# Moving six gathers and six adds from the end of a two-layer decoder kernel into its last expert pass, and reordering two steps of its mixers

## The reference, cut to what matters

```python
for l in range(2):
    hn = rmsnorm(h, norm1_g[l]);  u = hn @ w_in[l]                       # 1024 -> 1536
    pool = (window_means(u[:, :512]) - u[:, :512]) @ pool_w[l] * scale   # windows 2, 4, 8, 16
    v = u[:, 512:1024] * sigmoid(u[:, 1024:])
    conv = silu(layernorm(depthwise_conv31(v) + b)) @ conv_pw_w[l]
    h = h + concat(pool, conv) @ w_out[l]
    hn = rmsnorm(h, norm2_g[l])
    if l == 0: h = h + (silu(hn @ wg) * (hn @ wu)) @ wd                  # dense
    else:                                                               # top 2 of 8 experts
        h = h + sum(gate[e] * (silu(hn @ wg[e]) * (hn @ wu[e])) @ wd[e] for e in top2)
y = rmsnorm(h, final_norm_g)      # and the last 15 and 30 rows of the two mixers' inputs
```

## Time and profile before

| | us |
|---|---|
| median of three runs | 1496.43 |
| the profiled execution | 1495.54 |
| its span | 1493.8 |
| PE busy in the span | 1461.5 |
| DVE busy | 1182.0 |
| ACT busy | 915.1 |
| POOL busy | 202.1 |

### The profile page before, as it was taken

The page is one execution under the profiler, slowest core; times in us unless marked ns, Lnnn a source line. Parts: engine busy times, 40 slices in busy tenths (PEclk is TensorE's granted clock), DMA queues, the critical chain, the costliest instruction groups (busy, mean ns, idle before and its releaser), DMA issues.

```text
span 1493.8 us, 21275 instructions
## 1 busy us (share of the span) xinstructions
PE 1461.5 (98%) x7895; PEld 1263.8 (85%) x7895; DVE 1182.0 (79%) x976; ACT 915.1 (61%) x740; POOL 202.1 (14%) x224
## 2 busy tenths in 40 slices
PE   8999999999999999999999999999999999999995
PEld 7879999999979977888888888888888888888884
DVE  4888655544686688888888888888888888888887
ACT  4253433333224587777777777777777777777773
POOL 1465000002344047500000000000000000000002
PEclk9999999999999999999999999999999999999997
DMA  7556996353284399999999999999999999999993
GB/s 203 159 188 207 334 286 198 95 173 113 64 253 161 119 364 400 384 395 377 390 364 385 386 361 384 379 379 382 374 382 371 376 385 361 382 388 370 382 379 113
DMA packets 249680, 453.56 MB, mean 304 GB/s; under 512 B 9605, under 2 KB 99781, under 8 KB 249631
## 3 DMA queue, kind: packets, MB, share of 16 engines
q1 hardware_dynamic: 245056, 442.33, 83.4%
q0 software_dynamic: 2960, 9.73, 2.0%
q10 hardware_dynamic: 1615, 0.85, 0.2%
HBM read 426.51 MB, written 26.37 MB: 303 GB/s over the span
## 4 chain that ended last, share of the span: by engine, by line
PE 66%; DVE 2%; ACT 1%; issue 1%; DVEq 0%; ACTq 0%
PE ps L1676 21%; PE ps L1674 21%; PE ps L1675 21%; PE ps L2044 2%; ACT w_hi L512 0%; PE ps L2034 0%; PE ps L2023 0%; DVE w_lo L517 0%; PE ps L1921 0%; PE ps L1757 0%; DVE yt L1656 0%; PE ps L2112 0%; DVE w_lo L1312 0%; PE ps L2113 0%; PE ps L1872 0%
## 5 line engine op out<-in xcount | busy, mean ns | idle before, releaser
L517 DVE TENSOR_TENSOR w_lo<-raw,w_hi 128x2048 fp32r<-128x2048 f32 x336 | 764.5, 2290 | 117.6 <-ACT w_hi L512 116.3
L512 ACT ACTIVATE w_hi<-raw 128x2048 fp32r<-128x2048 f32 x334 | 639.5, 1915 | 123.4 <-PE ps L1676 122.2
L1676 PE MATMUL ps<-w_hi,xg_lo 128*128 128x512 f32 x896 | 351.4, 392 | 0.0
L1674 PE MATMUL ps<-w_hi,xg_hi 128*128 128x512 f32 x896 | 350.9, 392 | 0.0
L1675 PE MATMUL ps<-w_lo,xg_hi 128*128 128x512 f32 x896 | 350.7, 391 | 0.0
L1675 PEld LDWEIGHTS ps<-w_lo,xg_hi 128*128 128x128 f32 x896 | 168.3, 188 | 37.2
L1674 PEld LDWEIGHTS ps<-w_hi,xg_hi 128*128 128x128 f32 x896 | 168.3, 188 | 36.7 <-DVE w_lo L517 0.2
L1676 PEld LDWEIGHTS ps<-w_hi,xg_lo 128*128 128x128 f32 x896 | 168.3, 188 | 36.1
L1674 PE MATMUL ps<-x_hi,w_hi 128*128 128x336 f32 x580 | 186.3, 321 | 5.9 <-DVE x_lo L1176 2.5
L1675 PE MATMUL ps<-x_lo,w_hi 128*128 128x336 f32 x580 | 183.6, 317 | 0.0
L1676 PE MATMUL ps<-x_hi,w_lo 128*128 128x336 f32 x580 | 182.9, 315 | 0.0
(11 more groups left out here) (283 smaller groups left out, 1576.1 us busy)
## 6 DMA issues: line engine op xcount, KB each, us to landing
raw<-in_moe_w_gate_dram SPq DMA_DIRECT2D x112, 1024.0 KB, 7.2
raw<-in_moe_w_up_dram SPq DMA_DIRECT2D x112, 1024.0 KB, 7.4
raw<-in_moe_w_down_dram SPq DMA_DIRECT2D x112, 1024.0 KB, 7.3
raw<-in_w_in_dram SPq DMA_DIRECT2D x11, 1024.0 KB, 5.2
raw<-in_ffn_w_gate_dram SPq DMA_DIRECT2D x11, 1024.0 KB, 6.0
raw<-in_ffn_w_up_dram SPq DMA_DIRECT2D x11, 1024.0 KB, 6.4
raw<-in_w_out_dram SPq DMA_DIRECT2D x8, 1024.0 KB, 7.7
obuf<-ones SPq DMA_DIRECT2D x15, 512.0 KB, 7.9
```

The source lines that it names most:

```text
L512: nc.scalar.activation(hi, r, ACT.Copy).then_inc(hi_done, 1)
L517: nc.vector.tensor_tensor(lo, r, hi.bitcast(F32), ALU.subtract).then_inc(lo_done, 1)
L1674: nc.tensor.matmul(out, a_hi, b_hi, start=start, stop=False)
L1676: return nc.tensor.matmul(out, a_lo, b_hi, start=False, stop=stop)
```

## The change

There are three edits. First, SP no longer increments `o_early`; POOL itself waits for `o_stored` (with the number of overflow chunks read into a register), issues the six gathers, and then does the six multiplications by the gates and six additions to `yt`, each as an instruction of its own on 112 x 1024 elements; DVE's six `add_gathered` are gone. Second, both halves of the fourth sample part (`conv_samples(3)`) stand ahead of the split of the last `w_in` slot, and the split of the pool maps' weights (`S_POOL_W`) moves behind the centring. Third, PE does the first six of the eight contraction steps of both outputs of slot `S_OUT` ahead of the last two pool maps, and the last two steps behind them.

```diff
@@ sync, behind the last weight load
             sp.wait_ge(o_stored, n_pass * 16 + 16)
-            sp.sem_inc(o_early, 1)
             store_tiles(sp, 0)
@@ gpsimd, at the end of its program
+            n_over = pool.value_load(eids[0:1, 6:7], min_val=0, max_val=5)
+            pool.wait_ge(o_stored, n_over * 16 + (NE * 16 + 16))
+            pool.sem_inc(o_early, 1)
             pool.wait_ge(o_early, 1)
             for i in (0, 1):
                 for t in range(3):
                     gather_outputs(i, t, og_landed[i][t])
+            for i, gates in enumerate((out_gate[:, 0], early_gate)):
+                for t in range(3):
+                    pool.wait_ge(og_landed[i][t], 16)
+                    link(nc.gpsimd.tensor_scalar(og[:, i, t, :], og[:, i, t, :], gates[:, t:t + 1], None, ALU.mult))
+                    nc.gpsimd.tensor_tensor(yt[:, t, :], yt[:, t, :], og[:, i, t, :], ALU.add).then_inc(y_added, 1)
+                    pool.wait_ge(y_added, 3 * i + t + 1)
@@ vector, mixer_layer
                 pool_in(4, 1)
-                conv_samples(3, (0,))
+                conv_samples(3)
...
                 low_half(0, pool_half_lo)
                 low_half(1, lo_done)
                 split_at[0] = n + 1
-                conv_samples(3, (1,))
-                split_to(b + S_POOL_W)
                 dve.wait_ge(sums_done, SUMS[("mean", l)] + 1)
@@ vector, at the end
-            def add_gathered(i, t, gates):
-                dve.wait_ge(og_landed[i][t], 16)
-                if i:
-                    dve.wait_ge(y_added, t + 1)
-                nc.vector.scalar_tensor_tensor(yt[:, t, :], og[:, i, t, :], gates[:, t:t + 1], yt[:, t, :],
-                                               ALU.mult, ALU.add).then_inc(y_added, 1)
...
-            for t in range(3):
-                add_gathered(0, t, out_gate[:, 0])
-            out_low(0)
-            add_gathered(1, 0, early_gate)
-            out_low(1)
-            for t in (1, 2):
-                add_gathered(1, t, early_gate)
+            for i in (0, 1):
+                out_low(i)
             dve.wait_ge(y_added, 6)
@@ tensor, mixer_layer
+                split_ready(b + S_OUT)
+                w_hi_0, w_lo_0 = dense_slot(b + S_OUT, 256)
+                first_outs = [group(("wout", l, i)) for i in (0, 1)]
+
+                def first_part(ks):
+                    for k in ks:
+                        pe.wait_ge(evac, GROUP[("pool", l, k) if k < NG else ("pw", l, k - NG)] + 1)
+                        for i in (0, 1):
+                            cols = slice(P * i, P * (i + 1))
+                            ins = mm3(first_outs[i][:, 0:T], w_hi_0[:, k, cols], w_lo_0[:, k, cols], m_hi[:, k, :], m_lo[:, k, :],
+                                      k == M_ORDER[0], k == M_ORDER[-1])
+                            if k == M_ORDER[-1]:
+                                ins.then_inc(mm_done, 1)
+
+                first_part(M_ORDER[:2 + KC])
                 for g in POOL_ORDER[2:]:
                     pool_map(g)
+                first_part(M_ORDER[2 + KC:])
...
-                for s in range(4):
+                for s in range(1, 4):
...
-                            if s == 0 and i == 0:
-
-                                pe.wait_ge(evac, GROUP[("pool", l, k) if k < NG else ("pw", l, k - NG)] + 1)
...
-                    if l == 1 and s:
+                    if l == 1:
```

## The result

| | before | after |
|---|---|---|
| median of the runs, us | 1496.58 | 1512.85 (1511.61 to 1515.08) |
| ratio, 95% interval | | 1.0113 [1.0101, 1.0125] |
| the profiled execution, us | 1495.54 | 1511.61 |
| its span, us | 1493.8 | 1509.8 |

The account below looks back on a forecast made before the run. PE was taken to bound the expert passes, with DVE having 23.3 us in 200 to spare. Last pass 12.4, mixers 2.6 and end 0 took the profiled 1495.54 to 1510.5, a median of 1511.4 (own range 1506 to 1517).

Parts of the forecast that it names:

- The sign and the size: Whole kernel: slower, median 1511.4 us; chance of slower 0.88, same 0.06, faster 0.06.
- A pass bound by PE gives nothing back: Last expert pass: the 12.4 us that PE waits for delayed splits are lost in full.
- The main term: Last pass: POOL's 18.4 us of sums hold up DVE's splits, so PE waits 12.4 us (bounds 8 and 17).
- The gathers: Last pass: gathers moved there make weight slots land some 6.5 us late, stalling about 2.3 us alone (bounds 0 and 4).
- I add nothing for it: Last pass: the gathers' 2.3 us fall where DVE is late already, so they add nothing to the 12.4.
- Output slot: Mixers, output slot begun ahead: waits of 0.7, 0.7 and 2.1 us replace 1.06; loss 2.4 a layer (bounds 0.5 and 3.5).
- Sample part: Mixers, fourth sample part: PE's wait of 1.22 us goes; gain 1.1 us a layer (0.8 to 1.22).
- End: End of the kernel: removing DVE's six adds gains 0 (bounds: gain 0.4, loss 0), as they were hidden behind PE.
- Rival 1: Last pass: POOL loses every arbitration and works only in DVE's idle time; 1503.9 us; chance 0.11.
- Rival 2: Last pass: sums cost DVE next to nothing, the gathers' lateness decides; 1501.3 us; chance 0.08.
- Rival 3: Last pass: PE's clock falls to 1.2 GHz while it starves, some 15 us more; 1526 us; chance 0.07.
- Rival 4: Whole kernel: sums run beside DVE, weights land in time, mixers gain both waits, end 0.4; 1491.7 us; chance 0.06.

Follow-up runs that it names:

- adds_only: Kernel before plus six POOL additions of 112 x 1024 on free tiles in the last pass, no multiplications, gathers and DVE's adds at the end: 1503.69 us, ratio 1.0051.
- end_edit: Kernel before with the whole first edit (gathers and sums on POOL in the last pass, DVE's adds gone), mixers as before: 1505.72 us, ratio 1.0070.
- gathers_early: Kernel before with only the six gathers moved into the last pass, issued by POOL; DVE adds at the end as before: 1499.90 us, ratio 1.0039.
- half_gathers: Kernel before with three of the six gathers moved into the last pass, the other three at the end as before: 1495.38 us, ratio 0.9996.
- sums_only: Kernel before plus six multiplications and six additions by POOL on free tiles in the last pass, gathers and DVE's adds at the end: 1502.65 us, ratio 1.0051.
- mults_only: Kernel before plus six POOL multiplications on free tiles in the last pass, no additions, gathers and DVE's adds at the end: 1495.41 us, ratio 1.0000.
- paced: Kernel before with POOL issuing the six gathers one by one in the last pass, each behind a later split, sums on DVE at the end: 1497.78 us, ratio 1.0014.
- best: Kernel before with the changes of paced and fill2 together: 1494.58 us, ratio 0.9991.
- sample_edit: Kernel before with the second edit alone (fourth sample part whole ahead of the split, pool-map split behind the centring): 1496.14 us, ratio 1.0006.
- slot_edit: Kernel before with the third edit alone (36 matmuls of both outputs ahead of the last two pool maps): 1503.74 us, ratio 1.0048.
- fill_only: Kernel before with six matmuls of the first output ahead of the very last pool map, fourth sample part as before: 1493.71 us, ratio 0.9988.
- fill2: Kernel before with the second edit and six matmuls of the first output ahead of the very last pool map: 1492.86 us, ratio 0.9974.

## Why the prediction was right, point by point

**The sign and the size.** Slower, 1511.4 against 1512.85. "A pass bound by PE gives nothing back" is what carried it: the 12.3 us of the last pass are three quarters of the loss. That the sum came out as near as this is luck, twice: within the last pass, as told next, and outside it, where the mixers cost 3.1 us more than predicted and the start 1.6, against 2.9 less at 500 us and 1.2 less at the end.

**The main term was right in sum and wrong in its parts.** The prediction charged every POOL instruction to DVE in full, 18.4 us in 12 turns, for 12.4 of PE. Alone, the sums cost 7.8. The step that failed is "I charge every POOL instruction to DVE in full": it was drawn from one addition and holds for additions only. Additions were also sized low: 1.914 us from the earlier trace rows, against about 2.2 of standing still in adds_only. A multiplication, put at 1.15 us from another form's row, takes 2.85 at least (end_edit), and that did no harm only because it holds hardly anything up. The sentence on the Trainium skill's GPSIMD Engine Reference (section "Instruction dispatch", an estimate of 2.13 us) was the nearer one. The rule of the Trainium skill's SBUF — State Buffer (section "SBUF: two separate sides"), by which a GpSimd instruction that reads SBUF holds the port pair for its whole length, the trace bears out for the additions and not for the multiplications, which share 2.6 us with a split that is longer by 0.7.

**The gathers.** "A stall of about 2.3 us taken alone" measured 7.9 alone. The size that failed is the lateness: 6.5 us, taken from the scatters, against landings that rose from 8.5 to 19.0 in gathers_early, by 10.5. With that, 3.4 of slack and 0.5 to 1.4 of cover, the same working gives 5.7 to 6.6; PE's stops there are 4.86, and the clock added 3 behind them. "I add nothing for it" was half right: 4 of the 7.9 vanish when the sums run as well. Two mistakes of opposite sign, sums 4.6 too dear and gathers 5.6 too cheap, with 4.1 of overlap, made the sum look exact; the experiments, not the total, tell that.

**Output slot.** Right: three new waits of 0.87, 0.77 and 1.87 for 0.7, 0.7 and 2.1, and 2.85 us in a layer without a fall of the clock, against 2.4.

**Sample part.** The wait went as predicted (1.5 for 1.1), but nothing was gained. The step that failed is the one on what is late next: it placed the moved split by when PE needs that split, and did not see that DVE does it ahead of the statistics, so that PE gets their `scratch` no earlier than before (12.38 us behind the convolution, and 12.36 before). So the gain of 1.1 a layer is 0. No step of the prediction looked at the clock in the mixers either.

**End.** 0 was predicted (bounds: gain 0.4), and the end gave 1.2 after the change and 3.1 in end_edit. The statement "the adds that the change takes from DVE were already hidden" is true of the kernel before, where DVE waits 1.20 us for PE behind them; once PE comes earlier they are not, as half_gathers shows. What moved is PE, in two places. The placed products took 8.0 us before and 5.8 in end_edit, where the clock had not yet fallen (5.6 in half_gathers, and 8.0 again after the change). And PE's first stop behind its last weight matmul got shorter, which the profile puts to DVE's low half. It can't be that alone: before, that low half ended at 1472.33 (it starts at 1471.64 and lasts 0.69) and PE began at 1474.46. The stop is 0.49 to 0.99 us in four kernels whose gathers have landed by then (half_gathers, end_edit, gathers_early, after), and 1.5 to 2.9 in those that still have gathers in flight (2.11 before, 2.48 in sums_only, 2.56 in mults_only); but paced and best, with their gathers landed, show 1.82 and 2.27, the latter put to "issue". So what makes it long stays open.

**Rivals.** Rival 1, POOL starved, is true of the multiplications and of nothing else. Rival 2 falls with sums_only: the sums alone cost 7.8. Rival 3, the clock, came in small: 3.5 us at 0.51 in the last pass, and in the mixers. (Its price is also added up wrongly: 12 slots of 5.6 instead of 3.9 us are 20 us more and not 15.) Rival 4's conditions are refuted one by one: splits are held up, and `S_OUT + 1` is waited for.

## What to carry to other kernels

Before work goes from DVE to GpSimd beside a loop that DVE only just feeds, count the GpSimd instructions with two SBUF operands: here each addition stopped DVE's two-operand splits for about its length (some 2.2 us for 1024 columns), six multiplications by a scalar cost next to nothing, and six bunched additions cost more than six spaced ones. A transfer that is moved into a stage with full DMA engines has to be spread over it, so that each slot's lateness stays inside the slack of the engine that takes it up, and what then remains to be gained has to be looked for at the place that it left. When a wait of PE goes and nothing is gained, look for the next wait in a kernel where the clock doesn't hide it. To fill a wait, move the smallest piece that fills it: 6 matmuls gained 0.9 us a layer where 36 lost 2.85, most of it because the 36 had been the cover of the next split.

## What had not been expected of the hardware

- GpSimd's multiplication by a scalar from memory takes 2.87 us for 112 x 1024 when it meets one split (mults_only), and up to 6.90 when splits follow each other (after); in mults_only it holds a split up for 0.0 to 0.9 us. An addition of the same size takes 2.42 (the first of adds_only), and the split that meets it waits.
- Six gathers, 2.75 MB, raised the landing time of the weight slots to 20.0 us (after), where scatters of as many bytes raised it to 12.5.
- Stretches of 3.5 to 7 us at 1.2 GHz come and go between the profiled executions: at 445.5 in sample_edit, 449 in slot_edit and after, gone at 500 in after, fill_only and fill2, and behind stops of 3.25 to 4.94 us in the last pass (end_edit, gathers_early, after). Some differ with no edit ahead of them: end_edit has one at 90.7 that the kernel before has not. Where PE has no slack such a stretch cost 1.3 to 3 us, as much as the waits that were being edited; where it would have waited for DVE anyway, nothing.
